# Five in-projection pieces as plain fp32 products, and attention normalised on its outputs instead of on its maps

## What is computed

```
proj = h @ w_in                     # 1024 x 2080 columns, cut into 9 pieces by the kernel
# MLA, each head
p = softmax(mask(q k^T * scale));   out = p @ v
# differential attention, each head
p1, p2 = softmax(q1 k1^T ...), softmax(q2 k2^T ...)
o = (p1 - lam * p2) @ v
o = rms_norm(o, diff_subln, 1e-5) * (1 - lam_init)
```

## Time and profile before

| | |
|---|---|
| runs | 1291.13 us median of 3 (1289.16 to 1294.21) |
| profiled execution | 1294.05 us, span 1292.0 us |
| busy share | PE 96%, PEld 80%, DVE 79%, ACT 64%, POOL 4% |
| granted TensorE clock, mean | 0.974 |
| DMA | 349.65 MB, 271 GB/s mean |
| layer 0: in-projection / attention with output projection | about 15 to 79 us / 79 to 150 us |
| layer 1: the same | about 351 to 415 us / 415 to 484 us |

### The profile page before, as it was taken

One profiled execution on the slowest core, in us unless ns is written; L12 is line 12 of the kernel. 1 busy time (PEld: TensorE's weight loads), 2 busy tenths in 40 slices (PEclk: granted clock), 3 DMA queues, 4 the chain that ended last, 5 costly groups with the idle time before them and its releaser, 6 DMA issues.

```text
span 1292.0 us, 17786 instructions
## 1 busy us (share of the span) xinstructions
PE 1243.1 (96%) x6342; PEld 1037.4 (80%) x6342; DVE 1020.8 (79%) x1175; ACT 830.5 (64%) x906; POOL 46.8 (4%) x57
## 2 busy tenths in 40 slices
PE   6989899999898998999999999999999999999997
PEld 6966688888797676888888888888888888888885
DVE  4885465555678747889989989989989989989986
ACT  5556455544543745777777777777777777777774
POOL 2000000000000002000000000000000000000000
PEclk9979899999999897999999999999999999999999
DMA  9600655555462029999999999999999999999961
GB/s 299 207 1 1 201 196 180 181 194 195 119 200 94 1 96 374 376 375 370 351 369 372 350 366 369 352 367 371 350 366 373 351 366 370 350 366 373 351 233 49
DMA packets 184739, 349.65 MB, mean 271 GB/s; under 512 B 15063, under 2 KB 72981, under 8 KB 184692
## 3 DMA queue, kind: packets, MB, share of 16 engines
q1 hardware_dynamic: 182428, 341.22, 74.7%
q0 software_dynamic: 2064, 7.27, 1.5%
q10 hardware_dynamic: 200, 0.54, 0.1%
HBM read 346.91 MB, written 2.10 MB: 270 GB/s over the span
## 4 chain that ended last, share of the span: by engine, by line
PE 93%; DVE 3%; ACT 1%; DMA 1%; issue 1%; SPq 0%; POOL 0%; POOLq 0%; DVEq 0%
PE bank L1477 24%; PE bank L1479 23%; PE bank L1478 23%; PE bank L1742 6%; PE bank L1743 3%; PE bank L1808 1%; PE bank L1558 1%; DVE cv L1118 1%; PE bank L1555 1%; PE bank L1627 1%; DMA raw_a<-in_w_gate_dense 1%; PE bank L1560 1%; PE bank L1487 1%; ACT hi_ring L682 1%; PE bank L1774 1%
## 5 line engine op out<-in xcount | busy, mean ns | idle before, releaser
L1012 DVE TENSOR_TENSOR lo_ring<-raw_m,hi_ring 128x2048 fp32r<-128x2048 f32 x168 | 382.9, 2288 | 51.6 <-ACT hi_ring L688 51.5
L688 ACT ACTIVATE hi_ring<-raw_m 128x2048 fp32r<-128x2048 f32 x168 | 322.2, 1918 | 84.0 <-PE bank L1479 84.0
L1477 PE MATMUL bank<-hi_ring,hT 128*128 128x512 f32 (+2 forms) x896 | 336.2, 375 | 0.0
L1479 PE MATMUL bank<-hi_ring,hT 128*128 128x512 f32 (+2 forms) x896 | 329.0, 367 | 0.0
L1478 PE MATMUL bank<-lo_ring,hT 128*128 128x512 f32 (+2 forms) x896 | 328.5, 367 | 0.0
L1012 DVE TENSOR_TENSOR lo_ring<-raw_a,hi_ring 128x2048 fp32r<-128x2048 f32 x96 | 219.1, 2290 | 30.9 <-ACT hi_ring L688 30.9
L688 ACT ACTIVATE hi_ring<-raw_a 128x2048 fp32r<-128x2048 f32 x96 | 183.5, 1919 | 52.6 <-PE bank L1479 52.6
L1477 PEld LDWEIGHTS bank<-hi_ring,hT 128*128 128x128 f32 x896 | 169.3, 189 | 29.0 <-DVE lo_ring L1012 2.4
L1007 DVE TENSOR_TENSOR lo_ring<-raw_a,hi_ring 128x2048 fp32r<-128x2048 f32 (+2 forms) x59 | 131.3, 2228 | 77.2 <-ACT hi_ring L682 77.2
L1479 PEld LDWEIGHTS bank<-hi_ring,hT 128*128 128x128 f32 x896 | 169.2, 189 | 28.3
L1478 PEld LDWEIGHTS bank<-lo_ring,hT 128*128 128x128 f32 x896 | 169.5, 189 | 26.5
(11 more groups left out here) (288 smaller groups left out, 1471.1 us busy)
## 6 DMA issues: line engine op xcount, KB each, us to landing
raw_m<-in_w_down_exp SPq DMA_DIRECT2D x80, 1024.0 KB, 5.8
raw_a<-in_w_up_exp SPq DMA_DIRECT2D x48, 1024.0 KB, 6.0
raw_m<-in_w_gate_exp SPq DMA_DIRECT2D x48, 1024.0 KB, 5.6
raw_a<-in_w_gate_exp SPq DMA_DIRECT2D x40, 1024.0 KB, 5.7
raw_m<-in_w_up_exp SPq DMA_DIRECT2D x40, 1024.0 KB, 6.6
raw_a<-in_w_in SPq DMA_DIRECT2D x12, 1024.0 KB, 6.8
raw_a<-in_w_gate_dense SPq DMA_DIRECT2D x11, 1024.0 KB, 5.3
raw_a<-in_w_up_dense SPq DMA_DIRECT2D x11, 1024.0 KB, 5.5
```

The lines of the kernel that those rows point to most:

```text
L688: A(hi_of(NA + j), t, ACT.Copy).then_inc(hi_ready, 1)
L1012: V.tensor_tensor(lo_of(NA + j), expert_slot(i, j)[0], hi_of(NA + j).bitcast(F32), ALU.subtract).then_inc(lo_ready, 1)
L1477: M(o, lh, rh, start=start, stop=False)
L1479: return M(o, ll, rh, start=False, stop=stop)
```

## The change

Two parts.

1. Pieces 4 to 8 of each in-projection are no longer split. ACT writes an fp32 copy of the normed, transposed input (`hT_f`, eight activations of 128x256, at p = 1, into the memory of `xn`), and PE multiplies it with the raw weights in one plain fp32 product where there were three fp32r ones. The raw buffer of such a piece is free only when PE has used it. All later ring numbers move (`ring_no`). ACT and DVE then split at p = 0, 6 and 7 only (pieces 3, 9, 10), and the convolution taps go to pieces 2 to 5.

2. Attention maps are no longer normalised. In MLA the raw exponentials are transposed; PE adds, for each head, two products with a block of ones that put the row sums into the free half of the output bank; DVE takes the reciprocal of that half (128x256) and multiplies the head pair's output by it into `o_mla`. In differential slots ACT's `scale` goes away: the map stays e1 + ratio*e2 with ratio rebuilt as -lam*sum1/sum2, and since the RMS norm after it cancels a row's scale, only its epsilon must be scaled: POOL squares sqrt(64*1e-5)*sum1, spread over 64 columns (`sum_bc`), and PE adds it to the sum of squares with two products against the identity per head pair. The copies of transposed maps change engines: ACT does the differential ones, DVE the MLA ones.

```diff
+DIRECT = (4, 5, 6, 7, 8)
+NR = NA - LAYERS * len(DIRECT)
-N_CONST = 4
+N_CONST = 6
-TAPS_AT = [0, 0, 10, 5, 10, 11, 10, 9, 7]
+TAPS_AT = [0, 0, 16, 12, 14, 20, 0, 0, 0]
...
 # SP
             def load(n, src, view):
                 if n >= RAW_A:
-                    sp.wait_ge(lo_ready, n - RAW_A + 1)
+                    if n - RAW_A in direct_pieces:
+                        sp.wait_ge(piece_used, n - RAW_A + 1)
+                    else:
+                        sp.wait_ge(lo_ready, ring_no(n - RAW_A) + 1)
...
 # POOL
+            nc.gpsimd.memset(half_ones[:].rearrange("p (h d) -> p h d", h=3)[:, 0:3:2, :], 1.0).then_inc(const_set, 1)
+            nc.gpsimd.memset(half_ones[:, MV:2 * MV], 0.0).then_inc(const_set, 1)
...
+                pool.wait_ge(piece_used, in_done(l, NIN - 1))
+                for h in range(HEADS):
+                    pool.wait_ge(exp_done, UNITS * l + 2 * h + 1)
+                    nc.gpsimd.tensor_scalar(sum_eps[:, h, :], row_sum[:, 2 * h, :], (DV * LN_EPS) ** 0.5, None, ALU.mult
+                                            ).then_inc(sum_scaled, 1)
+                    pool.wait_ge(sum_scaled, HEADS * l + h + 1)
+                    if 3 * l + h // 2 >= 2:
+                        pool.wait_ge(o_ss_mm, 3 * l + h // 2 - 1)
+                    wide = sum_eps[:, h, :].unsqueeze(2).broadcast_to([P, TT, DV])
+                    nc.gpsimd.tensor_tensor(sum_bc[:, h // 2 % 2, :, h % 2, :], wide, wide, ALU.mult
+                                            ).then_inc(sum_rows, 1)
...
 # ACT
-                def scale(k):
-                    act.wait_ge(comb_done, HEADS * l + k + 1)
-                    u, e = units_of(k)[0], e_sb[:, k % 3, 0, :]
-                    A(e[:, 0:P], e[:, 0:P], ACT.Copy, scale=coef[:, u, 0:1])
-                    A(e[:, P:3 * P], e[:, P:3 * P], ACT.Copy, scale=coef[:, u, 1:2]).then_inc(scaled_diff, 1)
...
-                    if p < NIN - 1:
+                    if p == 0:
+                        split(n0 + 3)
+                    if p in (6, 7):
                         split(n0 + 3 + p)
+                    if p == 1:
+                        act.wait_ge(hTlo_done, KT * (2 * l + 1))
+                        for k in range(KT):
+                            A(hT_f[:, k, :], bank[k // 2][:, (k % 2) * T:(k % 2 + 1) * T], ACT.Copy,
+                              scale=vecs[:, V_ATTN + KT * l + k:V_ATTN + KT * l + k + 1]).then_inc(hTf_done, 1)
...
-                        act.wait_ge(pv_mm, SLOTS * l + 2 * j + 2)
-                        A(hT_hi[:, 2 + 5 - j, :], bank[O_BANK[j % 2]][:, 0:T], ACT.Copy).then_inc(cat_hi["mla"], 1)
-                    if HEADS <= k - 2 < SLOTS:
+                        act.wait_ge(mla_normed, 3 * l + j - 2)
+                        A(hT_hi[:, 2 + 5 - j, :], o_mla[:], ACT.Copy).then_inc(cat_hi["mla"], 1)
+                    if 0 <= k - 2 < HEADS:
                         copy_transposed(k - 2)
-                    if 2 <= k <= HEADS:
-                        scale(k - 1)
...
 # DVE (its split follows ACT's: p = 0, 6, 7)
-                    if k >= HEADS:
-                        coefs(V.reciprocal(coef[:, us[0]], row_sum[:, us[0]]))
-                        dve.wait_ge(coef_ready, cr[0])
-                        e = e_sb[:, k % 3, 0, :]
-                        V.tensor_scalar(e[:, 0:P], e[:, 0:P], coef[:, us[0], 0:1], None, ALU.mult)
-                        V.tensor_scalar(e[:, P:3 * P], e[:, P:3 * P], coef[:, us[0], 1:2], None, ALU.mult
-                                        ).then_inc(scaled_mla, 1)
-                        return
...
                     j = (k - 4) // 2
                     if k % 2 == 0 and 3 <= j < 6:
+                        dve.wait_ge(pv_mm, SLOTS * l + 2 * j + 2)
+                        if j == 3:
+                            dve.wait_ge(o_normed, 3 * l + 3)
+                        else:
+                            dve.wait_ge(mla_normed, 3 * l + j - 3)
+                        V.reciprocal(o_rs, bank[O_BANK[j % 2]][:, T:2 * T]).then_inc(mla_recip, 1)
+                        dve.wait_ge(mla_recip, 3 * l + j - 2)
+                        if 3 * l + j > 3:
+                            dve.wait_ge(cat_lo["mla"], 3 * l + j - 3)
+                        V.tensor_tensor(o_mla[:], bank[O_BANK[j % 2]][:, 0:T], o_rs, ALU.mult).then_inc(mla_normed, 1)
+                    j = (k - 5) // 2 if k % 2 else (k - 4) // 2
+                    if k in (11, 13, 14):
                         dve.wait_ge(cat_hi["mla"], 3 * l + j - 2)
...
 # PE
+                    direct = p in DIRECT
+                    if direct:
+                        raw, arrived, count = raw_slot(n)
+                        pe.wait_ge(arrived, count)
+                        pe.wait_ge(hTf_done, KT * (l + 1))
+                        wf = in_piece_view(raw, p)
...
+                                if direct:
+                                    r = M(b[0:cn, m * T:(m + 1) * T], wf[:, k, c0:c0 + cn], hT_f[:, k, :],
+                                          start=k == 0, stop=k == KT - 1)
+                                    continue
...
-                                r = mm3(b[:, t * 192:(t + 1) * 192], hT_hi[:, k, tok], hT_lo[:, k, tok],
-                                        wh[:, k, :], wl[:, k, :], k == 0, k == KT - 1)
+                                r = M(b[:, t * 192:(t + 1) * 192], hT_f[:, k, tok], wf[:, k, :],
+                                      start=k == 0, stop=k == KT - 1)
...
                 def transposes(k):
-                    wait_slot(scaled_diff, scaled_mla, k)
+                    if k < HEADS:
+                        pe.wait_ge(comb_done, HEADS * l + k + 1)
+                    else:
+                        pe.wait_ge(exp_done, UNITS * l + units_of(k)[0] + 1)
...
+                    if k >= HEADS:
+                        ones_of = half_ones[:, odd * MV:odd * MV + P]
+                        M(o[:, T:2 * T], ones_of, pt[:, 0:T], start=False, stop=False)
+                        r = M(o[:, T + P:2 * T], ones_of, pt[:, T:3 * P], start=False, stop=False)
...
-                        M(bank[O_BANK[j % 2]][:, T:2 * T], blocks, o_sq, start=True, stop=True).then_inc(o_ss_mm, 1)
+                        o = bank[O_BANK[j % 2]]
+                        M(o[:, T:2 * T], blocks, o_sq, start=True, stop=False)
+                        pe.wait_ge(sum_rows, HEADS * l + 2 * j + 2)
+                        for t in range(TT):
+                            r = M(o[:, T + t * P:T + (t + 1) * P],
+                                  sum_bc[:, j % 2, t].rearrange("p h d -> p (h d)"), ident, start=False, stop=t == 1)
+                        r.then_inc(o_ss_mm, 1)
```

More of the change, by code:

```diff
@@ L332, in build @@
         spare = xn[:].rearrange("p t d -> p (t d)")
+        hT_f = spare.rearrange("p (k t) -> p k t", k=KT)
         pt_sb = spare[:, 0:6 * P].rearrange("p (s n) -> p s n", s=2)
@@ L435, in build, with ring_no @@
         block = ctx.enter_context(nc.Block())
+        direct_pieces = {LAYER_PIECE0[l] + p for l in range(LAYERS) for p in DIRECT}
+        split_pieces = [n for n in range(NA) if n not in direct_pieces]
+        def ring_no(n):
+            return split_pieces.index(n) if n < NA else NR + n - NA
         def raw_slot(n):
@@ L552, in expert_loads @@
                     if first and j < RAW_A:
-                        sp.wait_ge(lo_ready, max(n for n in range(NA) if n % RAW_A == j) + 1)
+                        sp.wait_ge(lo_ready, ring_no(max(n for n in range(NA) if n % RAW_A == j)) + 1)
                     elif first and j < RAW_M:
@@ L747, in exponentials @@
                         e = e_sb[:, k % 3, i, :]
+                        sums = [row_sum[:, u, b:b + 1] if k < HEADS else None for b in range(2)]
                         A(e[:, 0:P], s_sb[:, u % 3, 0:P], ACT.Exp, scale=-1.0, bias=neg_max[:, u, 0:1],
-                          accum_out=row_sum[:, u, 0:1])
+                          accum_out=sums[0])
                         A(e[:, P:3 * P], s_sb[:, u % 3, P:3 * P], ACT.Exp, scale=-1.0, bias=neg_max[:, u, 1:2],
-                          accum_out=row_sum[:, u, 1:2]).then_inc(exp_done, 1)
+                          accum_out=sums[1]).then_inc(exp_done, 1)
                 def copy_transposed(k):
@@ L855, in _ @@
                             act.wait_ge(o_normed, 3 * l + j)
-                        A(o_rs, bank[O_BANK[j % 2]][:, T:2 * T], ACT.Ln, scale=1.0 / DV, bias=eps_ln[:]
+                        A(o_rs, bank[O_BANK[j % 2]][:, T:2 * T], ACT.Ln, scale=1.0 / DV
                           ).then_inc(o_ln, 1)
```

67 lines of the change are left out of this document (37 added, 30 removed).

## The result

The changed kernel takes 1303.04 us at the median of five runs (1299.81 to 1304.08), the kernel before 1291.13 (1289.16 to 1294.46). The ratio is 1.0084, with a 95% interval of 1.0069 to 1.0098, so the change costs some 9 to 13 us. A second set of six runs gave 1.0076 (1.0060 to 1.0092). The forecast was +7.1 us, 1298 against the median, in a range of 1286 to 1304. It is a loss of more than the 6.5 us that the prediction took for its border to "slower", to which it gave 0.50.

A forecast was written before the change was run, and what follows sets the result against it. PE was taken as the bound, with 93% of the chain of waits. Layer 0 at +2.95 and layer 1 at +4.15 gave +7.1 us: 1301.2 on the profiled 1294.05, 1298 against the median 1291.13; range 1286 to 1304.

The forecast's parts named there:

- In-projection: Pieces 4 to 8 on PE: plain products add 1.16 us to each of 4-6, save 0.18 on 7-8; +3.1 us a layer.
- The hole: PE's 4.61 us wait for DVE's row minima after the in-projection: 3.1 pay for the projection, -1.2 us is left.
- Differential slots: First values to first MLA scores: identity products add 0.86 and 0.43 us; with the hole, -0.3 and -0.8 by layer.
- I take each layer's own pattern: Differential slots: half clock throughout in layer 0, back at 432.4 in layer 1, so identity products cost 0.86 and 0.43 us.
- Rival A: Attention: clock stays high, MLA scores 7.0 us after first values; sum -2.6 us, 1288.5, or 1287 with short reciprocal; 27%.
- MLA slots: PE bound: sums of squares +0.86, ones products +3.9 a layer (0.65 in slot 11), shorter wait -0.85 us.
- each added product counts: MLA slots: PE is the bound, so two sums of squares add 0.86 us and six ones products 3.9.
- Reciprocal: DVE's 128x256 reciprocal in MLA, called r: taken as 1.4 us, 0.42 below, about 2.2 with eight passes.
- Rival B: DVE's reciprocal slower, r = 2.2: MLA wait stays whole, layer 1's last output piece 1.9 us late; +9.5, 1301; 15%.
- End of a layer: Last output piece: PE waits r - 0.35, 1.05 us in layer 1; in layer 0 hidden behind dense-piece loads.
- Rival C: Clock returns a slot later: one MLA slot at half speed in each layer, some 3 us each; +13, 1304; 9%.
- D: Hole does not close, minima held by something other than taps: up to +4.6 us a layer, 1303 and above; 4%.

The follow-up runs named there:

- the filled kernel: Changed kernel with unused 128x128x256 fp32 products (one, three, two) in PE's idle time, against the kernel before: 1296.77 us, ratio 1.0050.
- the copy experiment: Changed kernel with a same-shape copy replacing the 128x256 reciprocal: 1302.36 us, ratio 1.0087; with PE's idle time also filled by unused products: 1295.42 us, ratio 1.0032.
- the filled kernel before: Kernel before, attention and projection untouched, with unused 128x128x256 fp32 products in PE's idle time: 1285.92 us, ratio 0.9951.
- the second profile: Profiled execution of the changed kernel run again without edit: 1303.19 us; that set's median 1302.92 us, ratio 1.0076 against the kernel before.

## Why the prediction came out as it did

**In-projection: right.** Piece 8 ends at 81.55 (forecast 81.6). In the changed kernel's chain in order of time piece 6 takes 6.91 us and pieces 7 and 8 take 5.20 and 5.21 (forecast 6.92 and 5.16). A plain product has two records as forecast, and the later loads and activations cost nothing.

**The hole: right.** 4.61 became 0.71 us, the first values are at 87.87 against 87.5 forecast, -0.8 instead of -1.2.

**Differential slots: the step that failed.** "I take each layer's own pattern" took the length of the half-clock stretch for a property of the layer. It is one of the execution: layer 0 had 20 us of it in the profile before, 7 and 13 in the two profiles after, and the MLA scores came 3.3 and 0.3 us earlier. Layer 1 came nearer (-0.2 against -0.8). Rival A (the clock stays high) did not happen, but the filled kernel shows that its price was right: 8.3 us from the first values (88.28) to the MLA point (96.56), of which two unused products take 1.0, where the rival had 7.0 and some 0.4 to that second product.

**MLA slots: mechanism right, size short.** Measured +3.97 a layer from the MLA point to `w_pw`, forecast 0.86 + 5 x 0.65 - 0.85 = 3.26. The waits shrank from 1.25 to 0.82 instead of 0.40, since DVE's copy comes at 0.65 even with a short reciprocal, as the copy experiment showed. With the measured r the forecast's own formula (4.5 + r - 5.5) gives 0.75, near those 0.82, but by luck: the 0.65 does not hang on r. Most of the other 0.3 is that a short wait costs more than its bracket, which counts from the modelled end of the record before. From the slot's last transposes to the first output product PE takes 0.65 us (124.04 to 124.69) with the wait of 0.17, and before it took 0.25 (124.49 to 124.74). That "each added product counts" holds only while PE, and not DVE, is the last to be ready: in the experiment without the ones products 1.3 us a layer come back as waits for DVE.

**Reciprocal: too short, and between both rules.** r was taken as 1.4 from the rows of two and four elements and measured 1.75, 6.8 ns an element. The Trainium skill, VectorE: DVE Perf Modes (First, the fixed hardware budget) has an iterated divide with a repeat count of 8, from which I had estimated 2.2 us; the trace shows more than a plain pass (0.42 for the multiplication of that size) but less than that estimate. Rival B asked for the 2.2 and did not happen. The formula at the end of the layer, r - 0.35, gives 1.40 us, and the wait was 1.41.

**End of a layer: right for layer 1, half right for layer 0.** In layer 1 the stage from `w_pw` to the transposes costs +2.4, of it 1.41 + 0.65 by the forecast's terms; the rest is mostly the wait again, since PE's products on either side of it start 1.79 us apart (482.58 and 484.37) where they otherwise start 0.23 apart. In layer 0 it costs -0.3 against the profile before (forecast 0), but +1.45 between the filled kernels. The stage takes 22.8 us in all three profiles of the changed kernel (two plain, one filled), while in the seven profiles with the old attention it was anything from 21.2 to 23.1. ACT's wait for the first dense piece says why; below, the kernel before, the filled kernel before and the changed kernel.

```profile
146.09 1.92 ACT L682 ACTIVATE hi_ring<-raw_a 128x2048 fp32r<-128x2048 f32 x1 [4.56 <-DMA raw_a<-in_w_gate_dense]
...
140.19 1.92 ACT L682 ACTIVATE hi_ring<-raw_a 128x2048 fp32r<-128x2048 f32 x1 [2.77 <-DMA raw_a<-in_w_gate_dense]
...
145.93 1.91 ACT L713 ACTIVATE hi_ring<-raw_a 128x2048 fp32r<-128x2048 f32 x1 [0.86 <-DMA raw_a<-in_w_gate_dense]
```

Counted from `w_pw` the piece has landed and ACT starts on it after 14.8, 13.0 and 14.1 us. In each of the seven profiles with the old attention the transposes follow 8.3 us behind that start, so the load chain is what the stage goes by, as I had said, but the landing itself moved between 12.9 and 14.9 us. The changed kernel needs 22.8 for its own longer chain. The cover was whole in the execution on which I built the sum and 1.45 us short in the filled kernel before, where the load landed earlier.

**The sum and the median: right by luck in part.** Against the profile before, the change's first profile is +6.2, near the +7.1, but with the clock's early return in it: the second profile is +9.1. And I set the sum against a median 2.9 us lower than the profiled run as if the changed kernel's would stand the same way. Its median stands 2.8 us above its profiled run. Rival C had the clock coming back later as a loss that the change might bring. What was missing is that it comes back at different times in executions of either kernel, and that the profile before was at the unlucky end (0.974). The measured 1303 is also the figure of rivals C and D (1304, and 1303 and above), yet neither mechanism was there: both profiles have the full clock before the first MLA scores of either layer, and the hole closed. With idle time filled in both kernels the change costs 12.8 us: 7.4 for the MLA slots of both layers, 2.4 at the end of layer 1, 1.45 at the end of layer 0, and 1.6 in small terms of both signs, of which 1.3 is the clock behind layer 1's gathers.

What stays open: why the projection part is worth 4.3 us on top of the new attention (1.0117 to 1.0084) and 2 on top of the old; the intervals allow both to be about 3. Open too is whether the projection part gains anything once idle time is filled.

## What to carry to other kernels

Before building a sum on one profiled execution, compare its mean granted clock with that of the other runs: if it lies at the edge, every term taken from a half-clock stretch, and the step from profile to median, is off by some us. Where PE waits often for short times, unused products in its waits can be worth more than the waits, so price a change on kernels filled in this way, and split it: here five plain pieces gained 2 us, two gained 7, and the attention lost 15. Moving a normalisation from the maps to the outputs did not pay here: its sums were extra products on the bounding engine (3.3 us in each layer's slots, 2.0 of it on the path), and the scalings that it saved were on engines with time to spare.

## What the runs showed of the hardware

- The granted clock falls and comes back at different points of the same kernel: back at 94 us in one execution and at about 100 in another. Such 6 to 7 us cost 3 us.
- Products of 128x128x256 in fp32 into a free bank, some six to thirteen a layer, keep the granted clock at 1.00 in most of the stretches where it was 0.50, and the kernel gets 0.3 to 0.5% faster.
- A reciprocal of 128x256 from PSUM on DVE takes 1.75 us, a multiplication or copy of that shape 0.42.
- The first dense piece, loaded behind the same seven small loads, is taken up by ACT 12.9 to 14.9 us after the start of the product that lets the loads go, in seven profiles of kernels with the same attention.
